# A two-block model in one kernel: Fourier stage with tokens folded about token 128, and retention values and gates taken as 512 columns with tokens in the partitions

## The reference

```python
h   = modulate(rmsnorm(x), shift, scale)              # [256, 2048]; adaLN: shift, scale, gate = silu(c) @ ada_w + ada_b
q, k, v, ga, u, gb = split(h @ w_in)                  # w_in [2048, 10240]
# retention, head i: q, k 128 wide (axial rope), v and gate 256 wide, context state S of both directions
D   = gamma_up ** max(i - j, 0) * gamma_down ** max(j - i, 0)
o   = (q @ k.T * D) @ v + (q * up) @ S_f + (q * down) @ S_b      # [256, 256]
y_r = o / sqrt(mean(o * o, axis=-1) + eps) * silu(ga)
# Fourier, group g: u 256 wide
y_f = real(fft over tokens and over channels of u) / 256 @ fno_w[g] * silu(gb)
x   = x + gate * (concat([y_r, y_f]) @ w_out)
```

## Time and profile before

| | |
|---|---|
| median of 3 runs | 2867.1 us (2862.36 to 2867.46) |
| profiled execution | 2870.17 us, span 2868.5 us |
| PE / DVE / ACT busy | 95% / 61% / 45% |
| mean granted TensorE clock | 0.978 |
| HBM read, mean rate | 530.46 MB, 186 GB/s |
| retention units, about | 1050 to 1455 us of the span |
| Fourier units, about | 1455 to 1713 us |

### The profile page before, as it was taken

How to read it: one execution, slowest core, us unless ns; L and a number is a source line. 1 busy time by engine, 2 the same in 40 slices (tenths; PEclk the granted TensorE clock), 3 DMA queues, 4 the chain that set the end, 5 groups by cost and what they waited for, 6 DMA issues and landing times.

```text
span 2868.5 us, 49783 instructions
## 1 busy us (share of the span) xinstructions
PE 2737.6 (95%) x19249; PEld 2568.2 (90%) x19249; DVE 1763.1 (61%) x2244; ACT 1280.6 (45%) x1670; POOL 18.4 (1%) x33
## 2 busy tenths in 40 slices
PE   7999999998889799999999999999999999999997
PEld 7998789998777699999999987879999999999786
DVE  6777878777656755555556535456675454555544
ACT  5556444554443434443343334444444444444443
POOL 1000000000000000000000000000000000000000
PEclk9999999998889899999999999999999999999999
DMA  6565866655537365555548644547685555555554
GB/s 185 151 196 159 271 185 204 186 178 173 162 129 271 104 197 167 176 177 185 174 156 277 207 147 154 188 144 250 228 292 180 186 182 181 181 180 185 175 189 139
DMA packets 450700, 534.50 MB, mean 186 GB/s; under 512 B 32955, under 2 KB 343750, under 8 KB 449670
## 3 DMA queue, kind: packets, MB, share of 16 engines
q1 hardware_dynamic: 447840, 522.29, 57.5%
q0 software_dynamic: 2064, 10.11, 1.1%
q10 hardware_dynamic: 662, 0.25, 0.0%
HBM read 530.46 MB, written 2.10 MB: 186 GB/s over the span
## 4 chain that ended last, share of the span: by engine, by line
PE 82%; DVE 7%; ACT 3%; DVEq 3%; DMA 2%; issue 2%; ACTq 0%; SPq 0%
PE banks L1742 16%; PE banks L1744 16%; PE banks L1743 16%; PE banks L1753 8%; PE banks L1754 8%; PE banks L1755 8%; DVE w_lo L1159 3%; ACT w_hi L656 2%; PE banks L1991 1%; PE banks L2120 1%; PE banks L2137 1%; PE banks L1899 1%; DVEq L1150 1%; DMA w_raw<-in_od_w_in 1%; DMA w_raw<-in_l_w_in 1%
## 5 line engine op out<-in xcount | busy, mean ns | idle before, releaser
L1159 DVE TENSOR_TENSOR w_lo<-w_raw,w_hi 128x1024 fp32r<-128x1024 f32 (+2 forms) x848 | 974.5, 1160 | 834.1 <-ACT w_hi L656 814.0
L656 ACT ACTIVATE w_hi<-w_raw 128x1024 fp32r<-128x1024 f32 (+2 forms) x848 | 844.4, 1005 | 1088.5 <-PE banks L1744 606.1
L1742 PE MATMUL banks<-act_hl,w_hi 128*128 128x256 f32 x4304 | 1249.1, 290 | 36.0 <-DVE w_lo L1159 17.1
L1744 PE MATMUL banks<-act_hl,w_lo 128*128 128x256 f32 x4304 | 1226.0, 285 | 0.0
L1743 PE MATMUL banks<-act_hl,w_hi 128*128 128x256 f32 x4304 | 1225.9, 285 | 0.0
L1742 PEld LDWEIGHTS banks<-act_hl,w_hi 128*128 128x128 f32 x4304 | 832.9, 194 | 52.3 <-DVE w_lo L1159 18.7
L1743 PEld LDWEIGHTS banks<-act_hl,w_hi 128*128 128x128 f32 x4304 | 832.9, 194 | 3.8 <-issue 2.4
L1744 PEld LDWEIGHTS banks<-act_hl,w_lo 128*128 128x128 f32 x4304 | 832.5, 193 | 0.0
L1753 PE MATMUL banks<-w_hi,act_hl 128*128 128x512 f32 (+3 forms) x1440 | 509.5, 354 | 26.4 <-DVE x_res L1505 7.5
L1754 PE MATMUL banks<-w_lo,act_hl 128*128 128x512 f32 (+3 forms) x1440 | 506.9, 352 | 0.0
L1755 PE MATMUL banks<-w_hi,act_hl 128*128 128x512 f32 (+3 forms) x1440 | 506.2, 352 | 0.0
(11 more groups left out here) (270 smaller groups left out, 1586.5 us busy)
## 6 DMA issues: line engine op xcount, KB each, us to landing
w_raw<-in_od_w_in SPq DMA_DIRECT2D x256, 512.0 KB, 4.5
w_raw<-in_ev_w_in SPq DMA_DIRECT2D x256, 256.0 KB, 3.6
w_raw<-in_l_w_in SPq DMA_DIRECT2D x96, 512.0 KB, 4.3
w_raw<-in_l_w_in SPq DMA_DIRECT2D x128, 256.0 KB, 3.2
ada_ring<-in_ada_w SPq DMA_DIRECT2D x128, 256.0 KB, 4.3
w_raw<-in_l_w_out SPq DMA_DIRECT2D x64, 512.0 KB, 4.9
y_mix<-in_ada_w SPq DMA_DIRECT2D x128, 256.0 KB, 3.1
const_b<-in_ada_w SPq DMA_DIRECT2D x128, 256.0 KB, 4.5
```

Of the source, the lines that this page charges most:

```text
L656: last = nc.scalar.activation(dst(w_hi[:, p % RING, :]), src(w_raw[:, p % RING, :]), ACT.Copy)
L1159: last = tt(dst(w_lo[:, p % RING, :]), src(w_raw[:, p % RING, :]), dst(w_hi[:, p % RING, :]).bitcast(F32), ALU.subtract)
L1742: mm(out, hi, a[:, kt, 0:T], start=start, stop=False, skip_group_check=True)
L1744: return mm(out, lo, a[:, kt, 0:T], start=False, stop=stop, skip_group_check=True)
```

## The change

**Fourier.** The tokens are folded about token 128. After ACT has copied u out of bank A, DVE makes two tiles of 256 channels x 128 tokens: four_e = u[128+j] + u[128-j] and four_o = u[128+j] - u[128-j], at hook 0 (with a wait for that copy, and one for the last retention output). The columns step becomes 2 matmuls of 256 columns on four_e with the cosines, 2 on four_o with the sines, and 2 with the one column of token 0 as stationary operand, which are added into row 0 of the second. ACT copies 2 x 256 instead of 2 x 512 columns. The rows step contracts over 128 folded tokens, twice: 4 matmuls instead of 8, with a new constant dft_fold in the place of dft_ns. PE waits for the fold where it waited for both copies.

**Retention.** Values and gate of a head lie side by side in the loaded piece (256 columns each). They are now taken together by tokens, 512 columns into bank C for the first 128 tokens and bank B for the second; 6 matmuls take the place of 12. BANKS becomes (0, 2, 1, 3, 4). o is computed with tokens in the partitions, still with 8 matmuls of 256 columns. The mean of squares is then along the free axis: ACT squares the two halves with an accumulated sum (hook 9 instead of 11), DVE makes the mean (9 instead of 13), ACT the root of 2 numbers a partition (11 instead of 13), DVE the reciprocal of these and two products of 256 columns (11 instead of 14). PE transposes the result, four 128x128 (hook 12), and ACT copies it into yt and gives the signal y (hook 14). The ones-matmuls of hook 10 are gone.

```diff
-BANKS = {... "ret": (0, 2, 3, 4, 1), ...}
+BANKS = {... "ret": (0, 2, 1, 3, 4), ...}
@@ constants
-    ns = (-dsn).reshape(2, P, T).transpose(1, 0, 2).reshape(P, -1)
+    even, odd = dc[P:].copy(), -dsn[P:]
+    even[0] *= 0.5
+    odd[0] = dc[0]
+    ns = np.concatenate([even, odd], 1)
@@ ACT, ret
                     full(sc, "ret", i, 1)
                     copy(ret_qk, bank(A)).then_inc(s_free, 1)
-                    full(sc, "ret", i, 2)
-                    copy(ret_v, bank(C)).then_inc(s_free, 1)
                     for t in range(TT):
-                        full(sc, "ret", i, 3 + t)
+                        full(sc, "ret", i, 2 + t)
+                        copy(ret_vg[:, t, :], bank((C, B)[t])).then_inc(s_free, 1)
+                    for t in range(TT):
+                        full(sc, "ret", i, 4 + t)
...
-                    full(sc, "ret", i, 5)
-                    copy(ret_g, bank(B)).then_inc(s_free, 1)
...
+                if p == 9:
+                    sc.wait_ge(s["o"], i + 1)
+                    for t in range(TT):
+                        last = nc.scalar.activation(halves(ret_sq)[:, t, :], half_of(5, t), ACT.Square,
+                                                    accum_out=ret_stat[:, 0, t:t + 1])
+                    last.then_inc(s["sq"], 1)
                 if p == 11:
-                    sc.wait_ge(s["o"], i + 1)
-                    nc.scalar.activation(ret_sq, bank(5), ACT.Square).then_inc(s["sq"], 1)
-                if p == 13:
                     sc.wait_ge(s["mean"], i + 1)
-                    nc.scalar.activation(ret_r, ret_r, ACT.Sqrt).then_inc(s["root"], 1)
+                    nc.scalar.activation(ret_stat[:, 1, :], ret_stat[:, 1, :], ACT.Sqrt).then_inc(s["root"], 1)
+                if p == 14:
+                    sc.wait_ge(s["tokT"], i + 1)
+                    copy(yt[:, ds(2 * i, 2), :], halves(bank(6))).then_inc(s["y"], 1)
@@ DVE, ret
-                if p == 13:
-                    ve.wait_ge(s["sum"], i + 1)
-                    ts(ret_r, PS[:, 6, 0:T], 1.0 / T, EPS, ALU.mult, ALU.add).then_inc(s["mean"], 1)
-                if p == 14:
+                if p == 9:
+                    ve.wait_ge(s["sq"], i + 1)
+                    ts(ret_stat[:, 1, :], ret_stat[:, 0, :], 1.0 / T, EPS, ALU.mult, ALU.add).then_inc(s["mean"], 1)
+                if p == 11:
                     ve.wait_ge(s["root"], i + 1)
-                    nc.vector.reciprocal(ret_r, ret_r)
+                    nc.vector.reciprocal(ret_stat[:, 2, :], ret_stat[:, 1, :])
...
+                    for t in range(TT):
+                        last = stt(halves(ret_tok)[:, t, :], half_of(5, t), ret_stat[:, 2, t:t + 1],
+                                   ret_vg[:, t, T:2 * T], ALU.mult, ALU.mult)
+                    last.then_inc(s["tok"], 1)
@@ DVE, four
+                if p == 0:
+                    ve.wait_ge(S["ret"]["y"], COUNT["ret"] + 1)
+                    ve.wait_ge(s_free, bank_count("four", i, 1))
+                    u = halves(four_u)
+                    tt(four_e, u[:, :, P:T], u[:, :, P:0:-1], ALU.add)
+                    tt(four_o, u[:, :, P:T], u[:, :, P:0:-1], ALU.subtract).then_inc(s["folded"], 1)
@@ PE, project, ret
-                    for k in range(TT):
-                        r = tokens(half(C, k), slot, 256, 256, act, p, k, first and k == 0, last)
...
+                        r = tokens(bank((C, B)[k]), slot, 256, 512, act, p, k, first, last)
...
-                    return two(B, 512, 5)
@@ PE, ret
-                if p == 10:
-                    te.wait_ge(s["sq"], i + 1)
-                    for e in range(2):
-                        r = mm(PS[:, 6, 0:T], ones[:, :], halves(ret_sq)[:, e, :], start=e == 0, stop=e == 1,
-                               skip_group_check=True)
-                    r.then_inc(s["sum"], 1)
+                if p == 12:
+                    te.wait_ge(s["tok"], i + 1)
+                    for e in range(2):
+                        for t in range(TT):
+                            r = nc.tensor.transpose(PS[:, 6, e * T + t * P:e * T + (t + 1) * P],
+                                                    halves(ret_tok)[:, t, e * P:(e + 1) * P], ident[:, :])
+                    r.then_inc(s["tokT"], 1)
@@ PE, four
                 if p == 1:
-                    te.wait_ge(s_free, all_left("four", i))
+                    te.wait_ge(s["folded"], i + 1)
...
-                    for t in range(TT):
+                    for n, (part, first) in enumerate(((four_e, 0), (four_o, T))):
                         for c in range(2):
-                            r = mm(bank(4 + t), u[:, c, t * P:(t + 1) * P], dft[:, c, :], start=c == 0, stop=c == 1,
-                                   skip_group_check=True)
+                            r = mm(PS[:, 4 + n, 0:T], part[:, c, :], dft[:, c, first:first + T], start=c == 0,
+                                   stop=n == 0 and c == 1, skip_group_check=True)
+                    for c in range(2):
+                        r = mm(PS[0:1, 5, 0:T], u[:, c, 0:1], dft[:, c, 0:T], start=False, stop=c == 1,
+                               skip_group_check=True)
...
                     for e in range(2):
-                        for t in range(TT):
-                            mm(half(6, e), four_c[:, t, e * P:(e + 1) * P], dft[:, t, 0:T], start=t == 0, stop=False,
-                               skip_group_check=True)
-                            r = mm(half(6, e), four_c[:, t, T + e * P:T + (e + 1) * P], dft_ns[:, t, :], start=False,
-                                   stop=t == 1, skip_group_check=True)
+                        for n in range(2):
+                            r = mm(half(6, e), four_c[:, n, e * P:(e + 1) * P], dft_fold[:, n, :], start=n == 0,
+                                   stop=n == 1, skip_group_check=True)
@@ out2, DVE
+                    0: [step(four, 0, COUNT["four"] - 1)],
```

More of the change, by code:

```diff
@@ L206, in build @@
         scr_b = sb("scr_b", [P, 4608])
+        ret_stat = sb("ret_stat", [P, 3, TT])
         acc_x2 = sb("acc_x2", [P, ADA_N])
@@ L216, in build @@
         dft = const_b[:, 0:1024].rearrange("p (k n) -> p k n", k=2)
-        dft_ns = const_b[:, 1024:1536].rearrange("p (k n) -> p k n", k=2)
+        dft_fold = const_b[:, 1024:1536].rearrange("p (k n) -> p k n", k=2)
         rel_up = const_b[:, 1536:2048]
@@ L243, in bank, with half_of @@
             return PS[:, n, :]
+        def half_of(b, n):
+            return PS[:, b, n * T:(n + 1) * T]
         def halves(ap):
@@ L295, in build @@
             "ret": ("gate", "arg", "tables", "rot", "rope", "state", "state_sb", "scaled", "scores", "decayed",
-                    "o", "sq", "sum", "mean", "root", "y"),
-            "four": ("gate", "cols", "cols_sb", "rows", "rows_sb", "o", "y"),
+                    "o", "sq", "mean", "root", "tok", "tokT", "y"),
+            "four": ("gate", "folded", "cols", "cols_sb", "rows", "rows_sb", "o", "y"),
             "conv": ("y",),
@@ L893, in ret @@
                         copy(ret_vc[:, t * T:(t + 1) * T], ctx_v).then_inc(s_free, 1)
-                    full(sc, "ret", i, 5)
-                    copy(ret_g, bank(B)).then_inc(s_free, 1)
                 if p == 3:
                     nc.scalar.drain()
-                    nc.scalar.activation(ret_g, ret_g, ACT.Silu).then_inc(s["gate"], 1)
+                    nc.scalar.activation(ret_vg[:, :, T:2 * T], ret_vg[:, :, T:2 * T], ACT.Silu).then_inc(s["gate"], 1)
                     sc.wait_ge(s["arg"], i + 1)
@@ L926, in four @@
                     sc.wait_ge(s["cols"], i + 1)
-                    copy(four_c, PS[:, 4:6, :]).then_inc(s["cols_sb"], 1)
+                    copy(four_c, PS[:, 4:6, 0:T]).then_inc(s["cols_sb"], 1)
                 if p == 6:
@@ L1078, in four_and_mix @@
                     if p == 5:
+                        sc.wait_ge(S["ret"]["y"], COUNT["ret"] + 1)
                         mix_pair(i)
@@ L1868, in project @@
                         filled(r)
-                    if first:
-                        enter(stage, i, 2)
-                    for k in range(TT):
-                        r = tokens(half(C, k), slot, 256, 256, act, p, k, first and k == 0, last)
-                    if last:
-                        filled(r)
                     for k in range(TT):
                         if first:
-                            enter(stage, i, 3 + k)
-                        r = tokens(PS[:, 3 + k, 0:384], slot, 128, 384, act2, p, k, first, last)
+                            enter(stage, i, 2 + k)
+                        r = tokens(bank((C, B)[k]), slot, 256, 512, act, p, k, first, last)
                         if last:
                             filled(r)
-                    return two(B, 512, 5)
+                    for k in range(TT):
+                        if first:
+                            enter(stage, i, 4 + k)
+                        r = tokens(PS[:, 3 + k, 0:384], slot, 128, 384, act2, p, k, first, last)
```

(31 more changed lines are left out.)

14 lines of the change are left out of this document (6 added, 8 removed).

## The result

The changed kernel takes 2849.74 us (median of 5, 2844.07 to 2852.04), the kernel before 2867.1 (median of 5, 2862.36 to 2867.81): ratio 0.9938, interval 0.9927 to 0.995, so 17.4 us faster. I had said 2837.0 with a range of 2831 to 2848. The direction was right, the gain a little over half of the 30.1 us of the sum, and the time 1.7 us outside the range. Its runs also spread more than those of before, 8.0 us against 5.5. The profiled execution was the fastest of the five: 2844.07, span 2842.4, and more than its own stages explain lies outside them. Where out2's gate rows begin, behind Fourier, it is 20.3 us ahead of before, at the end 26.1; 1.9 of the 20.3 it had already at retention's first rotation (1041.69 against 1043.57), ahead of which only unit 0's projections were changed (0.5 us). From there to the gate rows it is 694.1 us against 712.5, so 18.4 less.

A forecast was written before the change was run, and what follows sets the result against it. PE (TensorE) was taken as the bound, busy throughout the retention and Fourier windows. Savings of 20.6 + 8.7 + 2.7 - 1.6 - 0.3 = 30.1 us from the median 2867.1 gave 2837.0 us, range 2831 to 2848.

The forecast's parts named there:

- 5a: Fourier units 1 to 4 with adaLN loads: later landings charged at 0.4 us a unit, 1.6 in all; upper bound 10.3.
- Part 4: New DVE and ACT work and moved waits, in retention and at the Fourier fold: under cover of PE, costing nothing.
- rival 1: Fourier units with adaLN: supply bounds them, 10.3 us lost instead of 1.6, so 2845.7 us; chance 0.16.
- part 1: Fourier columns and rows steps on PE: 2.58 us saved a unit, 20.6 us over 8 units.
- part 2: Retention values and gate on PE: 512-column matmuls at 0.227 us save 0.068 a piece, 8.7 us over 128 pieces.
- rival 2: Retention's wider matmuls bring little, 0.2337 us instead of 0.227: 5.1 us less gain, 2842 us; chance 0.11.
- Rival 5: Fourier columns step: the one-column matmuls are nearly free, giving 2831 us; chance 0.06.
- Part 3: Retention norm on PE: two ones-matmuls removed, four transposes added, 0.38 us saved in each of 7 units, 2.7 us.
- rival 3: Retention: DVE's new wait at piece 9 starves PE, making the kernel slower, 2873 us; chance 0.04.
- Part 5b: Retention-Fourier seam: squeezed unit's 0.38 us lost, 1.20 us idle stays in another form, 0.3 charged for later retention banks.

The follow-up runs named there:

- the later measurement: The changed kernel, unaltered, measured again on one chip beside the kernel before and one with copy and fold both moved: 2851.51 us, ratio 0.9945 to before.

## Why the prediction was wrong

**The step that failed is 5a.** "I charge 0.4 us a unit, 1.6": the four units with adaLN cost 127.3 us in the first profile and 130.0 in the second, against 4 x 30.2 = 120.8 at PE's pace, so 6.5 to 9.2 us. I had the loop, but two things about it were wrong. First, I gave the fold its own 0.7 us in it and no wait (Part 4: copy and fold over +1.5 us after bank A is full), and did not follow what stands ahead of the copy on ACT: w_hi 2, whose weights come round the same loop. In the old trace the copy begins at 1551.17, later than the 1550.8 at which I put the adaLN step behind it. So the loop was not 29.9 us long: the chain shows a lap of 32.16. The copy is a member of the loop, not a fixed time; moving it (8 us between the medians) and moving the fold (6 us) both shorten it. Second, I priced a PE wait at its length. After some waits the granted clock falls to its half level (1.81 and 3.17 us, but not 1.11 or 1.62), and the 1.7 us lost nearly doubles the first of these.

My rival 1 had this place. It bounded the loss at 10.3 us, and seven traces with the new Fourier stage and the waits unmoved lose 6.5 to 10.4. I gave it a chance of 0.16. Its sign, PE waiting for w_lo, did not come: PE waited for ACT's copy. Moving both waits is shown to bring the time back, on one chip and with intervals that do not overlap; for one move alone the runs of the changed kernel are those of other measurements. That the executions differ from each other by how late the loads land is not shown. It is argued from the 339 GB/s burst and from the spread, and with both moves the spread was 3.2 us once and 8.5 the other time.

By its own signs, too, the prediction was wrong: units without adaLN shrank by 2.29 us, not by 2.5 or more (part 1), and retention by 0.90, not by more than 1 us a unit (part 2).

**Part 2 was mis-sized:** 0.068 a piece predicted, 0.032 measured, 4.1 us instead of 8.7. The predicted lower bound (0.2337, 3.6 us) was nearly right; rival 2 had it. By the gap formula of the Trainium skill (TensorE: Matmul & The Clock Gate, Back-to-back issue gap) I had estimated 1.9; the traces show 4.1, and neither of my levels gives that either. What sets the level is open.

**Part 1:** 2.58 a unit predicted, 2.29 measured, 18.3 us instead of 20.6. The rows step and the full columns came as costed; for the one-column matmuls I had taken what a full one does, 0.43 each, as the upper end, and the two cost 0.27 more. Rival 5, that they are nearly free, is out.

**Part 3:** right, 0.39 against 0.38 a unit; the transposes in retention are issued 0.11 us apart. The Trainium skill (TensorE: Matmul & The Clock Gate, Part 4: PE-mode transpose) gives about 275 ns for one in a kernel; the trace shows that as the duration (0.272), not as the distance.

**Part 4:** right for retention. In no profile does PE wait more than 0.2 us in a retention unit, so rival 3 did not occur. Wrong for the fold ("Nothing directly"), as above.

**Part 5b:** right in size: PE's 1.20 us at Fourier unit 1 is 1.23 now, released by the copy instead of w_lo, and the wait for all retention banks grew from 0.34 to 0.56.

**Sum with measured terms:** 18.3 + 4.1 + 2.7 - 6.5 to 9.2 = 15.9 to 18.6. The first medians have 17.4; those of the later measurement have 13.4, which is 2.5 less than its own trace (9.2 lost) accounts for.

## What to carry to other kernels

When a stage is paced by PE while its loads are busy too (here a DMA share of 0.88), write the supply loop out as a ring of waits and ask of every new wait whether what it waits for is itself a member of the ring; a time copied from the old trace is not fixed then. A new wait on one engine belongs behind the work that others wait for: both repairs move one hook by one or two pieces, and together they bring the kernel from 2851.5 to 2837.3 us on one chip, of which the traces place 9.8 us in the stage. To see whether a stage runs in such a loop, look at whether the chain passes through PE there; its busy share was 95% before and after. And an idle PE can cost more than its idle time.

## What the runs showed of the hardware

- A stationary operand of one column made two F32 matmuls of 256 moving columns cost 0.27 us a unit more than one of 128 columns did. Its load began with its matmul, where a full one's began 0.22 us ahead.
- F32 transposes of 128x128 last 0.27 us and start 0.11 us apart.
- The distance between 512-column fp32r matmuls has two levels in out2, 0.227 and 0.2337 us, at a granted clock shown as 1.00; in retention it averages 0.232, and 384-column matmuls next to them go from 0.1735 to 0.177. Neither the columns' place in the slot nor the tile of the stationary operand brought the lower level to retention.
- After PE waits of 1.8 and 3.2 us the granted clock was at 0.50 for 3.4 us; after one of 1.11 us it was not, nor after one of 1.62 us in the same profile (a unit of 31.96 at 1.00). With both waits moved it fell after one of 1.21 us, and with the fold moved it did not after one of 1.66. So the length of the wait alone does not tell.
